# Summing the first modulation chunks in one PSUM region, with a ninth chunk and the squares added on VectorE

## What is computed

```python
s_c, s_cc = silu(c), silu(c_ctx)
for i in range(2):
    mx = split(s_c @ ada_w[i] + ada_b[i], 9)
    mc = split(s_cc @ ada_w[i] + ada_b[i], 9)
    x  = x  + 0.5 * mx[2] * swiglu(rms_norm(x,  g) * (1 + mx[1]) + mx[0])
    xc = xc + 0.5 * mc[2] * swiglu(rms_norm(xc, g) * (1 + mc[1]) + mc[0])
    ...                       # a mixer (pooling, then differential attention), a second swiglu step
```

## Time and profile before

| | us |
|---|---|
| median of three runs | 2895.75 |
| lowest and highest of the three | 2893.96, 2901.99 |
| the profiled execution's own time | 2896.53 |
| its span, from first to last instruction | 2894.9 |
| TensorE busy in the span | 2776.9 |
| VectorE busy | 2050.3 |
| ScalarE busy | 1008.1 |

### The profile page before, as it was taken

How to read it: one execution, slowest core, us unless ns; L and a number is a source line. 1 busy time by engine, 2 the same in 40 slices (tenths; PEclk the granted TensorE clock), 3 DMA queues, 4 the chain that set the end, 5 groups by cost and what they waited for, 6 DMA issues and landing times.

```text
span 2894.9 us, 49313 instructions
## 1 busy us (share of the span) xinstructions
PE 2776.9 (96%) x19386; PEld 2449.7 (85%) x19386; DVE 2050.3 (71%) x3072; ACT 1008.1 (35%) x1148; POOL 81.9 (3%) x154
## 2 busy tenths in 40 slices
PE   7999999999999999999999899998999999999999
PEld 5788877888878888788799899887799989986999
DVE  4877768867777777676666766656767767665677
ACT  3222224222232222233344444452143434443433
POOL 1000000000000000000000000000000000000000
PEclk9999999999999999999999999999999999997999
DMA  7544441443334454322245344421045454443344
GB/s 314 173 145 173 169 166 56 168 155 130 130 116 160 145 178 169 111 100 74 84 174 189 131 174 174 180 88 60 3 153 187 180 141 181 176 167 71 117 185 178
DMA packets 68848, 421.42 MB, mean 146 GB/s; under 512 B 7688, under 2 KB 8840, under 8 KB 26864
## 3 DMA queue, kind: packets, MB, share of 16 engines
q1 hardware_dynamic: 47888, 340.21, 31.8%
q0 software_dynamic: 20864, 79.83, 8.6%
HBM read 418.94 MB, written 1.07 MB: 145 GB/s over the span
## 4 chain that ended last, share of the span: by engine, by line
PE 86%; DVE 8%; issue 3%; ACT 2%; DMA 1%; DVEq 0%; SPq 0%; ACTq 0%
PE ps_o L2128 11%; PE ps_o L2129 10%; PE ps_o L2130 10%; PE ps_u L2128 7%; PE ps_u L2129 7%; PE ps_u L2130 7%; PE ps_g L2128 7%; PE ps_g L2129 7%; PE ps_g L2130 7%; PE ps_g L2143 2%; DVE wlo L1192 1%; PE ps_o L2348 1%; DVE tsq L1245 1%; ACT whi L709 1%; DVE scr L1387 1%
## 5 line engine op out<-in xcount | busy, mean ns | idle before, releaser
L709 ACT ACTIVATE whi<-wraw 128x2048 fp32r<-128x2048 f32 x314 | 598.9, 1911 | 788.2 <-PE ps_u L2130 382.2
L1192 DVE TENSOR_TENSOR wlo<-wraw,whi 128x2048 fp32r<-128x2048 f32 x314 | 710.9, 2287 | 153.0 <-ACT whi L709 152.8
L2128 PE MATMUL ps_o<-ah,wlo 128*128 128x256 f32 (+1 forms) x1408 | 464.3, 330 | 25.0 <-issue 15.5
L2128 PE MATMUL ps_g<-hh,wlo 128*128 128x256 f32 (+1 forms) x1464 | 463.3, 316 | 12.8 <-ACT tsq L824 7.4
L2128 PE MATMUL ps_u<-hh,wlo 128*128 128x256 f32 (+1 forms) x1464 | 461.9, 316 | 0.4 <-DVE wlo L1192 0.4
L2129 PE MATMUL ps_u<-hl,whi 128*128 128x256 f32 (+1 forms) x1464 | 462.0, 316 | 0.0
L2129 PE MATMUL ps_g<-hl,whi 128*128 128x256 f32 (+1 forms) x1464 | 462.0, 316 | 0.0
L2130 PE MATMUL ps_g<-hh,whi 128*128 128x256 f32 (+1 forms) x1464 | 461.9, 316 | 0.0
L2130 PE MATMUL ps_u<-hh,whi 128*128 128x256 f32 (+1 forms) x1464 | 461.8, 315 | 0.0
L2129 PE MATMUL ps_o<-al,whi 128*128 128x256 f32 (+1 forms) x1408 | 455.1, 323 | 0.0
L2130 PE MATMUL ps_o<-ah,whi 128*128 128x256 f32 (+1 forms) x1408 | 454.9, 323 | 0.0
(11 more groups left out here) (454 smaller groups left out, 3702.8 us busy)
## 6 DMA issues: line engine op xcount, KB each, us to landing
wraw<-in_W SPq DMA_DIRECT2D x315, 1024.0 KB, 4.8
scr<-in_ADA POOLq DMA_DIRECT2D x128, 512.0 KB, 3.9
big<-in_AW SPq DMA_DIRECT2D x4, 1024.0 KB, 16.1
scr<-in_AW SPq DMA_DIRECT2D x4, 1024.0 KB, 24.6
scr<-bias_rows POOLq DMA_DIRECT2D x8, 384.0 KB, 8.7
x<-in_XT POOLq DMA_DIRECT2D x1, 2048.0 KB, 13.1
x<-in_MEMT POOLq DMA_DIRECT2D x2, 1024.0 KB, 6.8
cst<-in_CST POOLq DMA_DIRECT2D x1, 1511.5 KB, 7.1
```

Source lines behind the costliest of these rows:

```text
L709: nc.scalar.activation(whi[:, n % SLOTS, :], wraw[:, n % SLOTS, :], ACT.Copy).then_inc(w_hi, 1)
L1192: tt_(wlo[:, n % SLOTS, :], wraw[:, n % SLOTS, :], whi[:, n % SLOTS, :].bitcast(f32), sub).then_inc(w_lo, 1)
L2128: mm(out, a[1], b[0], start=first, stop=False)
```

## The change

The eight raw chunks add up in one PSUM region instead of eight. `ada_sc` becomes a tile of eight variants, written by eight ScalarE instructions: variant n holds the two silu columns at rows 2n and 2n+1, zeros elsewhere, so chunk n lands in rows of its own of the same 128 x 256 region (`ADA_SUM[0]`). One copy on VectorE and one turn of two matmuls with `pick` widened from 2 to 16 columns replace eight of each.

A ninth chunk (blocks 16 and 17, part of the gate) is made the same way in a second region, `ADA_SUM[1]`. On TensorE its multiply stands between the turn of the eight and `ffn(0)`; its turn stands behind `first_halves`; its copy on VectorE behind the norm; the bias is added in `ada_late_part`, ahead of `ada_gate`. `ADA_PLAN[0]` goes from (8, 4) to (6, 4), so that two `ada_block`s ahead of the loop go; the rest of the plan covers the same blocks as before.

The squares are summed over d on VectorE (seven additions of 128 x 512), and TensorE runs one matmul with ones, after its fourth chunk. `keep_clock` goes with `norm(NTOK, part=0)`, which is no longer called on TensorE. ScalarE no longer waits for the last chunk before it takes up the norm.

x is loaded by SP ahead of all chunks; SP's order is then AW0 to AW3, W0, AW4, AW5, W1, AW6 to AW8, W2. The chunks' semaphores are grouped (0, 0, 0, 1, 1, 1, 2, 3, 4). POOL loads `CB` after the fifth chunk has been multiplied, the first blocks after the eighth, and `lamb` and `rel` behind the first step's blocks.

```diff
-ADA_FIRST = 8
-AW_GROUP = (0, 0, 1, 1, 2, 2, 3, 4)
+ADA_RAW = 8
+ADA_FIRST = ADA_RAW + 1
+AW_GROUP = (0, 0, 0, 1, 1, 1, 2, 3, 4)
-ADA_PLAN = ((8, 4), (8, 3), (2, 4))
+ADA_PLAN = ((6, 4), (8, 3), (2, 4))
...
+        ADA_SUM = [ps_o[:, 0, 0:256], ps_o[:, 1, 0:256]]
+        ADA_COLS = [ps_o[:, 2, 0:4 * ADA_RAW], ps_o[:, 3, 0:4]]
...
         def _(sp):
+            sp.dma_start(x[:], XT).then_inc(x_in, 16)
+            for n in range(4):
+                ada_chunk(n)
+            first_weights(0)
+            for n in (4, 5):
+                ada_chunk(n)
+            first_weights(1)
+            for n in (6, 7, 8):
+                ada_chunk(n)
+            first_weights(2)
...
         def _(pool):
-            pool.dma_start(x[:], XT).then_inc(x_in, 16)
             nc.gpsimd.memset(ada_sc, 0.0).then_inc(ad_zero, 1)
-            pool.dma_start(lamb[:], LAM).then_inc(lam_pm_in, 16)
-            pool.dma_start(rel, REL).then_inc(bias_in, 16)
-            pool.wait_ge(ad_turn, 1)
+            pool.wait_ge(ad_mm, 5)
             pool.dma_start(ada_c.rearrange("p v k -> p (v k)"), CB).then_inc(cb_in, 16)
+            pool.wait_ge(ad_mm, ADA_RAW)
...
         def _(act):
-            nc.scalar.activation(ada_sc[:, :, 0:2], V("c", 0, 16).rearrange("p (v k) -> p k v", v=2), ACT.Silu).then_inc(ad_silu, 1)
+            for n in range(ADA_RAW):
+                nc.scalar.activation(ada_sc[:, n, :, 2 * n:2 * n + 2], V("c", 0, 16).rearrange("p (v k) -> p k v", v=2), ACT.Silu).then_inc(ad_silu, 1)
-            act.wait_ge(ad_mm, ADA_FIRST)
...
         def _(dve):
-            for n in range(ADA_FIRST):
-                ada_out(n)
-                if n in (6, 7):
-                    split_lo(n - 6)
+            for d in range(1, KT):
+                dve.wait_ge(nm_sq, d + 1)
+                link(tt_(first(0), first(0), first(d), add))
+            for n in range(2):
+                split_lo(n)
             st["late"] = [2]
             norm(xs_, NTOK, A_mod(0, 0), B_mod(0, 0), "split", part=0)
+            ada_out(1)
             ffn(0, NTOK, gate(0, 0))
...
+            def ada_out(r):
+                dve.wait_ge(ad_mm, (ADA_RAW, ADA_FIRST)[r])
+                nc.vector.tensor_copy(lamb[:], ADA_SUM[r]).then_inc(ad_row, 1)
+            def ada_late_part():
+                dve.wait_ge(ad_turn, 2)
+                ps = ADA_COLS[1].rearrange("p (t v) -> p v t", v=2)
+                for v in range(2):
+                    ins = tt_(flat[:, 2 * ADA_RAW:ADA_B0, v], ps[:, v], V("ada_b", 2 * ADA_RAW, 2), add)
+                link(ins)
...
         def _(pe):
                 for k in range(KT):
                     rows = ADA_TILE[k % 4]
-                    ins = mm(ada_out_bank(n)[rows], ada_sc[:, k, :], w[:, k, :], start=k < 4, stop=k >= 4)
+                    ins = mm(ADA_SUM[r][rows], ada_sc[:, at, k, :], w[:, k, :], start=at == 0 and k < 4, stop=n >= ADA_RAW - 1 and k >= 4)
...
             pe.wait_ge(c_in, 32)
-            for n in range(ADA_FIRST):
+            pe.wait_ge(ad_silu, ADA_RAW)
+            for n in range(ADA_RAW):
                 ada(n)
-                if n:
-                    ada_turn(n - 1)
-                sum_squares(NTOK, max(0, 2 * n - 6))
-            norm(NTOK, part=0)
+                if n == 3:
+                    pe.wait_ge(dve_seq, KT - 1)
+                    mm(ps_g[:, 0, :], ones, tsq[:, 0:NTOK], start=True, stop=True).then_inc(nm_sum, 1)
+            ada_turn(0)
+            ada(ADA_RAW)
             ffn(0, NTOK)
```

More of the change, by code:

```diff
@@ L67, in constants @@
     s_, t_ = p[:, None], p[None, :]
-    pick = np.zeros((128, 2))
-    for v in range(2):
-        pick[v::32, v] = 1.0
+    pick = np.zeros((128, 2 * ADA_RAW))
+    for m in range(2 * ADA_RAW):
+        pick[m::32, m] = 1.0
     parts["pick"] = pick
@@ L381, in build @@
         v_d = cut(scr, 6144, 4096, "p (t n) -> p t n", t=4)
-        aw = [cut(big, CHUNK * n, CHUNK) for n in range(4)] + [cut(scr, 2 * D + CHUNK * n, CHUNK) for n in range(4)]
-        ada_sc = cut(rstd, 0, 32 * KT, "p (k m) -> p k m", m=32)
-        ada_rows = cut(hid, 0, 256 * ADA_FIRST)
+        aw = [cut(big, CHUNK * h, CHUNK) if h < 4 else cut(scr, 2 * D + CHUNK * (h - 4), CHUNK) for h in AW_HOME]
+        aw += [cut(scr, 0, CHUNK)]
+        ada_sc = cut(hid, 0, 2048, "p (n k m) -> p n k m", n=ADA_RAW, m=32)
         ada_junk = cut(scr, 0, 2 * D, "p (v k) -> p v k", v=2)
@@ L2278, in ada, with ada_turn @@
                 w = aw[n].rearrange("p (k n) -> p k n", n=256)
+                r, at = divmod(n, ADA_RAW)
                 for k in range(KT):
                     rows = ADA_TILE[k % 4]
[L2281 removed]
+                    ins = mm(ADA_SUM[r][rows], ada_sc[:, at, k, :], w[:, k, :], start=at == 0 and k < 4, stop=n >= ADA_RAW - 1 and k >= 4)
                 ins.then_inc(ad_mm, 1)
[L2284 to L2290 removed]
+            def ada_turn(r):
+                pe.wait_ge(ad_row, r + 1)
+                n = 2 * ADA_RAW if r == 0 else 2
+                for t in range(2):
+                    ins = mm(ADA_COLS[r][:, n * t:n * (t + 1)], lamb[:, 128 * t:128 * (t + 1)], C("pick", n), start=True, stop=True)
+                ins.then_inc(ad_turn, 1)
             def head_sums(nt, idle=2):
```

38 lines of the change are left out of this document (18 added, 20 removed).

## The result

The changed kernel takes 2880.57 us (median of 5 runs, 2877.08 to 2882.45); the kernel before, run beside it on the same chip, 2893.96 us (median of 5, 2888.75 to 2901.99). The ratio is 0.9949, with a 95% interval of 0.9930 to 0.9967: faster by 0.5%, 13.4 us between the medians and 10 to 20 us by the interval. The forecast was 2884.0, within 2879 to 2891.

The account below looks back on a forecast made before the run. The start was taken as bound by TensorE or VectorE's queue, whichever reaches the fifth down tile last. 9.8 us there plus 2.2 for the clock made 12.0: 2896.53 to 2884.5, less 0.8 for the median, so 2884, range 2879 to 2891.

Parts of the forecast that it names:

- What bounds the start: At the fifth down tile, whichever comes last, TensorE or VectorE's queue, sets the start; before the change it is VectorE.
- The loads: Group 1 lands at 29.5 us, x near 12, AW7 at 37.0, AW8 at 39.5 alone or 41.8 beside CB.
- The clock in the chunk work: Ahead of the stream, five chunks and one sum at the low level take 10.2 us; the stream starts at 44.0.
- first rival: Clock rises with the one full sum at 31 us; stream starts near 42.1, total 2881.5 us; chance 0.15.
- The low start of the stream: Feed-forward step begins at the low level for 4.8 us, losing 2.1; TensorE is through at 97.4.
- VectorE's queue: Ahead of the first residual addition, two fewer blocks save 4.6 us, late additions cost 0.3; done at 96.8.
- The clock behind the stall: Behind the stall at the fifth down tile, the clock stays up without it: 2.2 us saved.
- The sum: TensorE goes on 9.8 us earlier at the fifth down tile, plus 2.2 for the clock: 12.0 us.
- (2): POOL queue takes more than half, AW8 lands 2.5 us later, ninth chunk holds stream until 46.1: 2886 us; chance 0.15.
- (3): Block loads or CB come late, VectorE's chain stands at 68: only 4.3 and 2.2 us saved, 2889 us; chance 0.12.
- (4): Clock stays low through first_halves, all 192 matmuls low: slower than before, 2900 us; chance 0.04.

Follow-up runs that it names:

- less2: Kernel before with the seventh and eighth block ahead of the first loop not computed, their loads kept: 2887.18 us, ratio 0.9977.
- sum_early: Changed kernel with the one matmul of ones for the squares moved one chunk earlier, behind the third chunk: 2879.27 us (1 run).
- less1: Changed kernel with the sixth block ahead of the loop not computed: 2877.99 us (1 run).
- cb_late: Changed kernel with the load of CB issued behind the eighth chunk instead of the fifth: 2877.72 us (1 run).
- less1_warm: Changed kernel with the sixth block not computed and one unread 512-column matmul ahead of the ninth chunk: 2872.75 us (1 run).
- x_pool: Changed kernel with x loaded on POOL's queue instead of at the front of SP's: 2877.04 us (1 run).
- turns_back: Changed kernel with two unread matmuls of 2 columns behind each of the first seven chunks: 2886.28 us (1 run).
- before_sq: Kernel before with the squares added on VectorE and summed by one matmul behind the fifth chunk, turns kept: 2890.28 us, ratio 0.9988.
- plan8: Changed kernel without the ninth chunk, with plan (8, 4) and its two blocks back ahead of the loop: 2887.74 us, ratio 0.9978.
- sums8: Changed kernel with the eight sums of squares back on TensorE behind the fourth chunk, VectorE's additions out: 2891.34 us (1 run).
- again: Changed kernel run once more with no edit: 2879.40 us, ratio 0.9953.

## Why the prediction was right, point by point

**What bounds the start** held. VectorE's queue decided before (less2: 6.6 us for two blocks) and still does, by half a us: its first residual is done at 94.13, TensorE's side is through at 93.71. Where AW8 came late TensorE's side took over (sum_early, less1: no stall).

**The loads** held where the SP queue is alone: group 1 at 29.42 (said 29.5), x at 12.02 (12), AW7 at 36.88 (37.0). That they match to 0.1 us is in part luck: over the ten executions with x in front on SP's queue group 1 came between 27.4 and 29.9, and I had allowed 0.5. AW8 was there at 39.89; I had said 39.5 alone and 41.8 beside `CB`. Equal sharing of the rate was too dear for it. The runs show 9.9 us behind the fourth chunk with `CB` late (cb_late), and 11.5, 11.9, 11.2, 10.5, 9.9 and 10.1 where `CB` was issued 3.9, 4.9, 5.2, 5.3, 5.8 and 6.2 us behind it (sum_early, less1_warm, less1, the changed kernel twice, x_pool): in these single executions an early `CB` went with an AW8 up to 2 us late, a late one with none, if not in strict order. The Trainium skill (DMA: Bandwidth & Descriptors, Queues, rings and completion order) lets each DMA engine go round between its queues packet by packet; that `CB` slowed AW8 by 2 us in one execution and not at all in the next isn't in it, and what sets the share no run here shows.

**The clock in the chunk work** is the step that failed. I read 13 us of chunks without a rise and a rise behind 3.76 us of full sums, and put the low level down to the 32-wide shape. The two differed in something else as well: between the chunks of before stand turns of two columns. So the 13 us weren't chunk work alone. With tiny matmuls put back in the turns' places, and nothing else, all chunks stay slow (turns_back); without them the clock rises in chunk work alone (sum_early); with turns and without the full sums it stays low to the end (before_sq). So the sum of 10.2 us for five chunks and one sum became 8.5, and the turn 0.62 instead of 1.01. The eight chunks were done at 37.95 (said 39.9) and the stream began at 41.64 (said 44.0). The first rival's course came about, but not by its mechanism: it wanted the full sum to raise the clock, and in sum_early the clock rose in the chunks before that sum, and again in the chunks behind the pause. The page that it leaned on, of the Trainium skill (TensorE: Matmul & The Clock Gate, Part 1), says that sustained matmul activity releases the gate. The unbroken chunk work agrees with it. turns_back doesn't, if activity is read from the profile: the engine reads as busy for 14.78 of 15.00 us and stays slow.

**The low start of the stream** was right in kind and too large: I took 4.8 us at the low level and 2.1 us lost. After, the stream was slow from 41.64 to 43.51, eight matmuls, some 0.8 us lost. The ninth chunk ahead of it is matmul work too. Where AW8 came later (less1), it lasted to 45.6. I had taken TensorE's side to be the later one by 0.6 us (97.4 to 96.8); it is VectorE's, by 0.5.

**VectorE's queue** held. From the first block to the first residual it takes 94.13 - 59.50 = 34.63 us; before, 107.12 - 68.03 = 39.09. That is 4.46 less; I had said 4.3.

**The clock behind the stall** held: from the fifth tile to the gate matmul 5.60 us instead of 7.65, 2.05 (said 2.2); less2 (2.1) and plan8 show it from both sides.

**The sum** was 12.0 and came out as 15.0: the fifth tile 13.0 us earlier instead of 9.8, and 2.05 for the clock instead of 2.2. All of the miss of 3.0 lies ahead of the stream and at its start. The measured median, 2880.57, is 3.4 below the forecast, outside my own give or take 3 and 0.9 from the first rival's 2881.5; the range holds it because it took in the rivals. Counted from the five-run median of the kernel before, the same 12.0 would have said 2882.0; of the 3.0 us missed at the gate matmul these medians show 1.4 (13.4 for 12.0), the later ones 2.4 (14.4). That the time came so near the forecast is in part luck.

**Parts.** Undone alone, the sums on VectorE cost 5.9 us (sums8), the absence of turns between the chunks 7.0 (turns_back), the two blocks 6.8 (plan8): 19.7 together, and more than the 15.0 of the whole. They overlap, and not at the two blocks: with the sums or the turns put back VectorE still comes last at the fifth tile (a stall of 1.5 and 0.2 us), since its queue starts later with the norm. The overlap is between the sums and the turns: beside the turns, the single sum brought 3.3 us at the gate matmul and not 5.9 (before_sq). That fits, as it also took away the full sums behind which the clock rose in the kernel before; no run splits the overlap further. The root and the reciprocal ahead of the last chunk's end, 3.2 us of the stream's 8.4, have no run of their own; before_sq has them behind it still.

**The rivals.** (1) is told above. (2), a late AW8, is real but small: in sum_early and less1 it cost 1.1 to 1.2 us at the gate matmul, and in the changed kernel nothing, as VectorE has the last word. (3), late block loads, did not come: VectorE had its first block at 59.50. (4), the clock low through `first_halves`, did not come either: 1.9 us, at most 4.2 (less1).

**Beyond this change.** No variant is clearly faster than the changed kernel: VectorE's side and TensorE's are too near each other for one to be worth moving. By sum_early and less1, cb_late and a full matmul ahead of the ninth chunk would guard about 1 us against a late AW8; no run shows more. A version of the kernel before with all its turns behind the last chunk, which would show the turns' share there alone, wasn't tried: two engines would have touched one PSUM bank without an order between them.

## What to carry to other kernels

Where a stream starts late, look at what TensorE does just ahead of it by the time of equal instructions, not by its busy share: small matmuls sprinkled between larger ones can cost nearly as much again through the clock as by their own length (in turns_back the eight chunks took 6.6 us more, 3.7 of them for the tiny matmuls themselves), and gathered into one turn at the end they cost 0.6 us here. Taking work from a start-up pays only up to the engine that comes second, so work out both sides, and shorten both. And compare two traces at a fixed piece of work behind the change, counted from the same landing: here that put the gate matmul of the five executions with the changed kernel's queues on VectorE and AW8 in time within 0.1 us (70.3 to 70.4), where spans and single times scattered by several.

## What the runs showed of the hardware that was not expected

- Two matmuls of 2 columns (4 records, 1.0 us) between chunks of eight 32-wide ones (16 records) keep TensorE at 1.2 GHz (1.94 us a chunk, in turns_back to the ninth). The same chunks without them reach 2.4 GHz (1.07 us). The rise comes at differing points: the first three chunks took between 4.08 and 5.35 us in the ten executions without turns, and 5.35 is the low level throughout (3.64 for two and 1.70 more).
- The granted clock of a stretch reads 1.00 while its matmuls run at the pace of the low level (and turns_back above), and from 20 to 24 us of the changed kernel, whose first three chunks were slow for most of their time. After the column's first fall it agrees with the durations there: 0.50 from 30 to 33 us (the fourth chunk and the sum), 1.00 from 34 to 39, 0.50 from 41 to 43. The kernel before reads 1.00 from 17.5 to 45 us, though it was slow for two thirds of that, and 0.50 from 107 to 110, behind the stall. Ahead of a trace's first fall the time of a known instruction tells the level, the column does not.
- The clock is low again soon after it was high: in the changed kernel the eighth chunk ran at the high level from 36.88, then came a pause of 0.55 us, the turn and a pause of 0.78 us, and the ninth chunk at 39.89 took 1.82 us. With a pause of 0.24 us in the second place (cb_late, again) it took 1.07. The length of a pause doesn't settle it alone: behind the same 1.06 us ahead of the stream, the stream ran at the low level for 3 us in again and at the high level from its start in cb_late; their granted clock from 40 to 41 us reads 0.69 and 1.00.
- The first landing of this program varies by up to 2.5 us from one execution to the next, and moves all that follows with it.
